# Four norms summed and rooted on four columns, tokens on partitions, in place of full 128x512 tiles

## The chip, the core and the metric

The kernel runs on one NeuronCore of one Trainium2 chip. The metric is the device time of one execution in microseconds (us). Before the change the median of three executions is 3365.46 us (3362.30 to 3369.93). The profiled execution itself took 3365.46 us, of which the profile's span covers 3363.7 us.

## What is computed

The reference is a stack of two equal layers and one further block over 512 tokens of width 1024, in float32. The change touches one place that each of the two layers passes once: the norms behind the attention heads.

```python
for i in range(DEPTH):                      # DEPTH = 2
    x = x + 0.5 * swiglu(rmsnorm(x, ffn1_norm[i]), ...)
    h = rmsnorm(x, mix_norm[i]) @ w_in[i]
    y_mla  = mla_mixer(...)                 # 8 heads, 512 channels out
    y_conv = silu(layernorm(depthwise_conv(u, 31 taps), ln_g, ln_b))   # 256 channels
    y_hy   = hyena_mixer(...)               # 256 channels
    y = concatenate([rmsnorm(y_mla, g[:512]), rmsnorm(y_conv, g[512:768]), rmsnorm(y_hy, g[768:])])
    x = x + y @ w_out[i]
    x = x + 0.5 * swiglu(rmsnorm(x, ffn2_norm[i]), ...)

def rmsnorm(x, g):
    return x * rsqrt(mean(x * x, axis=-1) + 1e-6) * g
```

So four norms stand here: the variance of the layer norm, and the mean squares of the hyena, the convolution and the attention outputs. In each, one number per token is needed, which is then applied to every channel of the token.

## The kernel before

Channels lie on the 128 partitions and the 512 tokens along the free axis: a tile is 128x512, and `y` has eight such tiles (0 and 1 convolution, 2 and 3 hyena, 4 to 7 attention). A sum over channels is thus a sum over partitions, which TensorE makes with a matrix of ones.

Each engine has its own program, written out by hand in its order; the only coupling is semaphores. `after(sem, k)` and `wait_ge` wait for a count. A wait holds everything that stands behind it on the same engine.

Weights come as 128x1024 blocks by DMA, GpSimd (POOL) splits each into a high and a low half (L452, L455), and TensorE multiplies in three passes (L506, L510, L511: `product`). `x_hi`/`x_lo` hold the two halves of the right-hand operand. `out_pair(half, pair)` is one such block of the output projection: 24 matmuls. Half 0 writes banks 4 to 7, half 1 banks 0 to 3. The pairs take, in turn, tiles 0 and 1 of the scaled hyena output (pair 0), the convolution (pair 1) and the attention (pairs 2 and 3) as `y_hi`, `y_lo`.

The order around the change, for one layer, on TensorE: the last part of head 6 with `conv_mean`; `hyena_sum` (two matmuls of the ones matrix with squared tiles, 128x512, into bank 0); `head(7, conv_variance, nothing)`, that is the two matmuls of the variance, then the transposes of the probabilities (`turn`, L800) and the products with the values (`mix`, L811); `run_idle(6)`, twelve matmuls whose result nobody reads (L859); `out_pair(0, 0)`; the sums of the convolution's and the attention's squares (`ones_sum`, L820, two and four matmuls); `out_pair(1, 0)`; and the six other pairs.

ScalarE squares the tiles, takes the square root of each 128x512 sum from its bank (`root`, L1428, and L1506) into `mix_rms` or `late_rms` (the memory of `key_rope`), copies the turned probabilities (`turned`, L1419), rounds scaled tiles to `y_hi` (`round_off`, L1434), and applies the SiLU of the convolution (L1513). Exponential, square root and SiLU need different function tables, and the table is loaded where the first user stands, behind that user's wait.

VectorE inverts the whole 128x512 root (`inverted`, L2116), scales (`scale_tiles`, L2105) and takes the remainders (`remainders`, L2111) that `out_pair` waits for by `norm_split`.

The same kernel already has, in its input projection, a narrow form of a norm: `latent_sums` (L891, data as the stationary operand against one column of ones, so that tokens come out on partitions, 128x4), a root and a reciprocal of 128x4, and `latent_spreads` (L899, an identity matmul of a broadcast column that spreads it back over a 128x128 square).

## Time and profile before

| | |
|---|---|
| median of 3 executions | 3365.46 us |
| profiled execution | 3365.46 us, span 3363.7 us |
| TensorE (PE) busy | 3224.4 us, 96% |
| VectorE (DVE) busy | 1827.7 us, 54% |
| ScalarE (ACT) busy | 739.2 us, 22% |
| GpSimd (POOL) busy | 1833.5 us, 55% |
| mean granted TensorE clock | 0.988 of full speed |

The busy share is an average over the whole span. The place that changes lies at 632 to 688 us for the first layer and at 1694 to 1750 us for the second. In the timeline a row is a run of like instructions: start, length, engine, line, operation, what it writes and reads, how many records, and in brackets how long the engine stood idle before it and for whom. A float32 matmul leaves two records. The granted clock is 1.00 for 2.4 GHz and 0.50 for 1.2 GHz.

### The profile page before, as it was taken

What the parts mean: (1) busy time and instruction counts of PE and PEld (TensorE: products, weight loads), DVE (VectorE), ACT (ScalarE), POOL (GpSimd) and SP (SyncE); (2) the same over time, 40 slices, a digit from 0 to 9 for tenths busy, and PEclk for the clock granted to TensorE, in tenths of its full rate; (3) what the DMA queues carried; (4) which work ended last, traced back from release to release, by engine and by line L of the source; (5) the groups of instructions that cost most, each with busy time, mean ns of one, the idle gap of its engine ahead of it and who ended that gap; (6) DMA issues with size and microseconds to landing.
All of it is one profiled execution on the core that took longest, in us unless ns stands there. A gap on an engine that the chain in (4) does not pass through costs nothing.

```text
span 3363.7 us, 44081 instructions
## 1 busy us (share of the span) xinstructions
PE 3224.4 (96%) x14534; PEld 2575.2 (77%) x14534; DVE 1827.7 (54%) x1997; ACT 739.2 (22%) x1248; POOL 1833.5 (55%) x1026
## 2 busy tenths in 40 slices
PE   8999998899999999998889999999999999999998
PEld 6788875578888778876557888788777877888886
DVE  7661378663313765138755331586768886753312
ACT  2110125422201111013532220112122322222200
POOL 5556651066666656653036666644455455666665
PEclk9999999999999999999999999999999999999999
DMA  4222320022333322231012232322222222223232
GB/s 159 76 88 94 113 82 20 12 83 96 97 96 103 111 76 92 96 112 51 13 38 94 94 100 94 122 76 68 64 85 69 76 69 70 94 92 96 97 97 81
DMA packets 77431, 281.26 MB, mean 84 GB/s; under 512 B 9383, under 2 KB 9767, under 8 KB 76777
## 3 DMA queue, kind: packets, MB, share of 16 engines
q1 hardware_dynamic: 74016, 268.58, 24.8%
q10 hardware_dynamic: 3272, 10.79, 0.9%
q8 instruction: 89, 1.46, 0.2%
q14 instruction: 54, 0.43, 0.0%
HBM read 277.24 MB, written 2.10 MB: 83 GB/s over the span
## 4 chain that ended last, share of the span: by engine, by line
PE 78%; DVE 15%; issue 4%; ACT 2%; DVEq 0%; DMA 0%; ACTq 0%; SPq 0%
PE bank L506 23%; PE bank L511 23%; PE bank L510 23%; DVE short L1926 1%; PE bank L641 1%; PE bank L726 1%; DVE x_lo L1706 1%; DVE y L1958 1%; DVE square_sum L1716 1%; DVE xbc L2267 1%; DVE scaled L2105 1%; PE bank L791 1%; PE bank L800 1%; DVE att_qk L2203 0%; DVE reach L2360 0%
## 5 line engine op out<-in xcount | busy, mean ns | idle before, releaser
L452 POOL TENSOR_SCALAR w_hi<-raw 128x1024 fp32r<-128x1024 f32 x504 | 555.6, 1102 | 1456.3 <-PE bank L506 1449.3
L455 POOL TENSOR_TENSOR w_lo<-raw,w_hi 128x1024 fp32r<-128x1024 f32 x504 | 1265.0, 2510 | 42.0
L506 PE MATMUL bank<-x_hi,w_hi 128*128 128x512 f32 x2896 | 1150.8, 397 | 48.7 <-DVE x_lo L1706 20.4
L511 PE MATMUL bank<-x_hi,w_lo 128*128 128x512 f32 x2896 | 1133.5, 391 | 0.0
L510 PE MATMUL bank<-x_lo,w_hi 128*128 128x512 f32 x2896 | 1132.9, 391 | 0.0
L506 PEld LDWEIGHTS bank<-x_hi,w_hi 128*128 128x128 f32 x2896 | 547.4, 189 | 184.2 <-issue 67.4
L510 PEld LDWEIGHTS bank<-x_lo,w_hi 128*128 128x128 f32 x2896 | 547.6, 189 | 114.7 <-issue 4.1
L511 PEld LDWEIGHTS bank<-x_hi,w_lo 128*128 128x128 f32 x2896 | 546.9, 189 | 115.6
L506 PE MATMUL bank<-hidden_hi,w_hi 128*128 (+1 forms) x880 | 342.3, 389 | 0.0
L511 PE MATMUL bank<-hidden_hi,w_lo 128*128 (+1 forms) x880 | 342.3, 389 | 0.0
L510 PE MATMUL bank<-hidden_lo,w_hi 128*128 (+1 forms) x880 | 342.3, 389 | 0.0
L1726 DVE SCALAR_TENSOR_TENSOR x<-bank,x 128x512 f32<-128x512 f32 x64 | 43.3, 687 | 547.6 <-PE bank L511 547.1
L1742 DVE TENSOR_TENSOR up<-bank,rstd 128x512 f32<-128x512 f32 x110 | 76.1, 692 | 338.7 <-PE bank L511 329.9
L1746 DVE TENSOR_TENSOR hidden_lo<-hidden,hidden_hi 128x512 f32 (+1 forms) x110 | 155.2, 1411 | 116.1 <-ACT hidden_hi L1275 116.1
L506 PEld LDWEIGHTS bank<-hidden_hi,w_hi 128*128 128x128 f32 x880 | 165.2, 188 | 34.6
L511 PEld LDWEIGHTS bank<-hidden_hi,w_lo 128*128 128x128 f32 x880 | 165.2, 188 | 34.3
L510 PEld LDWEIGHTS bank<-hidden_lo,w_hi 128*128 128x128 f32 x880 | 165.2, 188 | 34.0
L1275 ACT ACTIVATE hidden_hi<-hidden 128x512 f32 (+1 forms) x110 | 69.6, 633 | 432.5 <-DVE hidden L1744 432.5
L1259 ACT ACTIVATE x_hi<-x,gains 128x512 fp32r<-128x512 f32 x56 | 40.3, 720 | 516.5 <-DVE x L1726 516.2
L1744 DVE TENSOR_TENSOR hidden<-gate_silu,up 128x512 f32<-128x512 f32 x110 | 126.1, 1147 | 38.8 <-DVE up L1742 26.5
L1273 ACT ACT_TABLE_LOAD x68 | 87.2, 1283 | 239.5 <-DVE gate L1740 239.5
L1273 ACT ACTIVATE gate_silu<-gate 128x512 f32<-128x512 f32 x110 | 69.6, 633 | 218.2 <-DVE gate L1740 217.4
(383 smaller groups left out, 3228.4 us busy)
## 6 DMA issues: line engine op xcount, KB each, us to landing
raw<-in_w SPq DMA_DIRECT2D x504, 512.0 KB, 3.7
dft<-in_dft ACTq DMA_DIRECT2D x2, 1536.0 KB, 6.7
out<-x SPq DMA_DIRECT2D x4, 512.0 KB, 2.6
mask<-in_mask ACTq DMA_DIRECT2D x1, 1536.0 KB, 7.3
x<-in_x SPq DMA_DIRECT2D x2, 512.0 KB, 5.0
x<-in_x SPq DMA_DIRECT2D x1, 1024.0 KB, 7.4
filt_cos<-in_dft_filter ACTq DMA_DIRECT2D x2, 512.0 KB, 6.6
filt_sin<-in_dft_filter ACTq DMA_DIRECT2D x2, 512.0 KB, 7.8
```

The lines of the kernel that those rows point to most:

```text
L452: nc.gpsimd.tensor_scalar(w_hi[:, s % 2, :], raw[:, s, :], 1.0, 0.0, ALU.mult, ALU.add).then_inc(w_rounded, 1)
L455: nc.gpsimd.tensor_tensor(w_lo[:, s % 2, :], raw[:, s, :], w_hi[:, s % 2, :].bitcast(F32), ALU.subtract).then_inc(w_split, 1)
L506: first = nc.tensor.matmul(out, hi_w, hi, start=start, stop=False)
L510: nc.tensor.matmul(out, hi_w, lo, start=False, stop=False)
L511: return nc.tensor.matmul(out, lo_w, hi, start=False, stop=stop)
L1259: nc.scalar.activation(x_hi[:, m, :], x[:, m, :], ACT.Copy, scale=g).then_inc(x_rounded, 1)
L1273: nc.scalar.activation(gate_silu[:], gate[:], ACT.Silu).then_inc(gate_activated, 1)
L1275: nc.scalar.activation(to, hidden[:], ACT.Copy).then_inc(hidden_rounded, 1)
L1726: nc.vector.scalar_tensor_tensor(x[:, m, :], banks[b][:], coef, x[:, m, :], ALU.mult, ALU.add).then_inc(x_updated, c.add(x_updated))
L1742: link(nc.vector.tensor_tensor(up[:], bank[2 * b + 1][:], rstd[:], ALU.mult), pair_free)
L1744: link(nc.vector.tensor_tensor(hidden[:], gate_silu[:], up[:], ALU.mult), hidden_ready)
L1746: link(nc.vector.tensor_tensor(to_lo, hidden[:], to_hi.bitcast(F32), ALU.subtract), hidden_split)
```

## The change

The sums are made with the data as the stationary operand against one column of ones (`column_sums`), so that a sum is 128x4 and not 128x512. Root and reciprocal work on 128x4. Identity matmuls (`spread_root`) spread the reciprocal over a bank. For hyena and the layer norm VectorE reads that bank; for the two later norms ScalarE first copies the banks to `mix_rms` and `late_rms` (`root_taken`). The twelve idle matmuls go. Two one-element activations load the SiLU and the square root table at other places than before.

```diff
-        latent_root = sb("latent_root", [P, TT], F32, mix_mem)
+        latent_root = sb("latent_root", [P, 2 * TT], F32, mix_mem)
...
+            def column_sums(to, tiles):
+                for t in range(TT):
+                    for i, tile in enumerate(tiles):
+                        last = nc.tensor.matmul(bank[to][:, t:t + 1], tile[:, t * P:(t + 1) * P], ones[:, 0:1],
+                                                start=i == 0, stop=i == len(tiles) - 1)
+                return last
+
+            def spread_root(n, to, first=0):
+                after(latent_inverted, n)
+                for t in range(TT):
+                    last = nc.tensor.matmul(bank[to][:, t * P:(t + 1) * P],
+                                            latent_root[:, first + t:first + t + 1].broadcast_to([P, P]), ident[:],
+                                            start=True, stop=True)
+                last.then_inc(latent_spread, 1)
...
             def conv_variance():
                 after(ln_squared, 2)
-                ones_sum(HYENA_BANKS[0], conv_squares).then_inc(ln_sum, 1)
+                column_sums(HYENA_BANKS[0], conv_squares).then_inc(ln_sum, 1)
+                spread_root(3, HYENA_BANKS[1])
...
-                ones_sum(HYENA_BANKS[1], hyena_squares).then_inc(norm_sum, 1)
+                column_sums(HYENA_BANKS[1], hyena_squares).then_inc(norm_sum, 1)
...
-                head(7, conv_variance, nothing)
-
-                run_idle(6, SCORE_BANKS[0], probs_ready, 32)
+                head(7, conv_variance, lambda: spread_root(4, HYENA_BANKS[0]))
+
                 after(norm_split, 3 + 2)
-                after(norm_rms, 4)
+                after(probs_ready, 32)
                 out_pair(0, 0)
                 after(norm_squared, 3 + 7)
-                ones_sum(TURN_BANKS[0], conv_squares).then_inc(norm_sum, 1)
-                after(norm_squared, 3 + 5)
-                ones_sum(TURN_BANKS[1], mla_squares, 0, 3)
+                column_sums(TURN_BANKS[0], conv_squares).then_inc(norm_sum, 1)
                 after(norm_squared, 3 + 8)
-                ones_sum(TURN_BANKS[1], mla_squares, 3, 4).then_inc(norm_sum, 1)
+                column_sums(TURN_BANKS[1], mla_squares).then_inc(norm_sum, 1)
+                spread_root(5, TURN_BANKS[0])
+                spread_root(6, TURN_BANKS[1], TT)
                 after(mixed_copied, 8)
-                after(norm_rms, 6)
+                after(norm_rms, 8)
                 out_pair(1, 0)
...
-                def root(at, width, to):
-                    act.wait_ge(norm_sum, c.next(norm_sum))
-                    nc.scalar.activation(to[:], bank[at][:], ACT.Sqrt, bias=eps[:], scale=1.0 / width
-                                         ).then_inc(norm_rms, 1)
+                def root(at, width, done, first=0):
+                    act.wait_ge(done, c.next(done))
+                    nc.scalar.activation(latent_root[:, first:first + TT], bank[at][:, 0:TT], ACT.Sqrt, bias=eps[:],
+                                         scale=1.0 / width).then_inc(norm_rms, 1)
+
+                def root_taken(n, at, to):
+                    after(latent_spread, n)
+                    nc.scalar.activation(to[:], bank[at][:], ACT.Copy).then_inc(norm_rms, 1)
...
                 turned(7, 2)
                 turned(7, 3)
+                nc.scalar.activation(exp_warm[:], eps[:], ACT.Silu)
                 round_off([y_hi[k] for k in (0, 1)])
                 for i in range(CT):
                     act.wait_ge(norm_scaled, c.next(norm_scaled))
-                    nc.scalar.activation(y[:, i, :], scaled[:, i, :], ACT.Silu,
+                    nc.scalar.activation(y[:, i, :], y[:, i, :], ACT.Silu,
...
                 mla_square(3)
                 c.add(mixed_copied, 8)
-                root(TURN_BANKS[0], CW, mix_rms)
-                root(TURN_BANKS[1], T, late_rms)
+                nc.scalar.activation(exp_warm[:], eps[:], ACT.Sqrt)
+                root(TURN_BANKS[0], CW, norm_sum)
+                root(TURN_BANKS[1], T, norm_sum, TT)
+                root_taken(5, TURN_BANKS[0], mix_rms)
+                root_taken(6, TURN_BANKS[1], late_rms)
...
                 head(6, branches_done, hyena_done, centre)
-                inverted(mix_rms)
-                scale_tiles([y[:, 2 + i, :] for i in range(CT)], OUT_NORM + 2, mix_rms)
-                inverted(late_rms)
+                latent_inverse()
+                dve.wait_ge(latent_spread, c.next(latent_spread))
+                scale_tiles([y[:, 2 + i, :] for i in range(CT)], OUT_NORM + 2, bank[HYENA_BANKS[1]])
+                latent_inverse()
+                dve.wait_ge(latent_spread, c.next(latent_spread))
+                scale_centred()
                 remainders((0, 1))
-                scale_tiles([conv_acc[:, i, :] for i in range(CT)], LN_G, late_rms)
                 mixed(7)
+                latent_inverse()
+                latent_inverse(TT)
...
-                inverted(mix_rms)
+                dve.wait_ge(norm_rms, c.next(norm_rms))
                 scale_tiles([y[:, i, :] for i in range(CT)], OUT_NORM, mix_rms)
                 remainders((2, 3))
-                inverted(late_rms)
+                dve.wait_ge(norm_rms, c.next(norm_rms))
                 scale_tiles([y[:, 4 + i, :] for i in range(2)], OUT_NORM + 4, late_rms)
```

The first place is TensorE at the start of head 7. Before (L820 is `ones_sum`, L800 `turn`):

```order
L820 MATMUL bank<-square,ones 128x512 [waits norm_squared]
L820 MATMUL bank<-square,ones 128x512
L820 MATMUL bank<-short,ones 128x512 [waits ln_squared]
L820 MATMUL bank<-short,ones 128x512
L120 REGISTER_ALU
L800 MATMUL bank<-ident,probs 128x128 [waits probs_scaled]
```

And now (L854 is `column_sums`, L862 `spread_root`):

```order
L854 MATMUL bank<-ones,square 128x1 [waits norm_squared]
L854 MATMUL bank<-ones,square 128x1 x7
L854 MATMUL bank<-ones,short 128x1 [waits ln_squared]
L854 MATMUL bank<-ones,short 128x1 x7
L120 REGISTER_ALU
L862 MATMUL bank<-ident,latent_root 128x128 [waits latent_inverted]
L862 MATMUL bank<-ident,latent_root 128x128 x3
L120 REGISTER_ALU
L800 MATMUL bank<-ident,probs 128x128 [waits probs_scaled]
```

Two matmuls of 512 columns have become eight of one column, and a wait for VectorE with four identity matmuls now stands in front of the transposes.

The second place is TensorE ahead of the first pair of the output projection (L506). Before (L811 is `mix`, L859 `run_idle`):

```order
L811 MATMUL bank<-square,mla_v 64x256 [waits turned_copied]
L811 MATMUL bank<-square,mla_v 64x256
L859 MATMUL bank<-spectrum,ones 64x256 [waits probs_ready]
L859 MATMUL bank<-spectrum,ones 64x256 x11
L120 REGISTER_ALU
L120 ISA [waits norm_split]
L120 REGISTER_ALU [waits norm_rms]
L506 MATMUL bank<-x_hi,w_hi 128x512 [waits w_split]
```

And now:

```order
L862 MATMUL bank<-ident,latent_root 128x128 [waits latent_inverted]
L862 MATMUL bank<-ident,latent_root 128x128 x3
L120 REGISTER_ALU
L811 MATMUL bank<-square,mla_v 64x256 [waits turned_copied]
L811 MATMUL bank<-square,mla_v 64x256
L811 MATMUL bank<-square,mla_v 64x256 [waits turned_copied]
L811 MATMUL bank<-square,mla_v 64x256
L120 REGISTER_ALU
L120 REGISTER_ALU [waits norm_split,probs_ready]
L506 MATMUL bank<-x_hi,w_hi 128x512 [waits w_split]
```

The filler is gone, and the second spread stands between the last transposes and the last products.

The third place is TensorE between the first pair and the second. Before:

```order
L820 MATMUL bank<-short,ones 128x512 [waits norm_squared]
L820 MATMUL bank<-short,ones 128x512 x2
L120 REGISTER_ALU
L820 MATMUL bank<-short,ones 128x512 [waits norm_squared]
L120 REGISTER_ALU [waits mixed_copied]
L120 REGISTER_ALU [waits norm_rms]
L506 MATMUL bank<-x_hi,w_hi 128x512 [waits w_split]
```

And now:

```order
L854 MATMUL bank<-ones,short 128x1 [waits norm_squared]
L854 MATMUL bank<-ones,short 128x1 x15
L120 REGISTER_ALU
L862 MATMUL bank<-ident,latent_root 128x128 [waits latent_inverted]
L862 MATMUL bank<-ident,latent_root 128x128 x3
L120 REGISTER_ALU
L862 MATMUL bank<-ident,latent_root 128x128 [waits latent_inverted]
L862 MATMUL bank<-ident,latent_root 128x128 x3
L120 REGISTER_ALU [waits mixed_copied,norm_rms]
L506 MATMUL bank<-x_hi,w_hi 128x512 [waits w_split]
```

Ahead of both pieces stand the sums of the convolution, two matmuls before and eight now.

## Rows read from the trace of the kernel before

**Rows 1.** The page: busy times by engine, and the chain that ended last.

```profile
PE 3224.4 (96%) x14534; PEld 2575.2 (77%) x14534; DVE 1827.7 (54%) x1997; ACT 739.2 (22%) x1248; POOL 1833.5 (55%) x1026
...
PE 78%; DVE 15%; issue 4%; ACT 2%; DVEq 0%; DMA 0%; ACTq 0%; SPq 0%
```

**Rows 2.** Timeline of TensorE, layer one; the last row is layer two.

```profile
636.02 3.75 PE L820 MATMUL bank<-square,ones 128*128 128x512 f32 x4 [3.58 <-ACT square L1497]
639.56 2.86 PE L820 MATMUL bank<-short,ones 128*128 128x512 f32 x4
642.26 1.04 PE L800 MATMUL bank<-ident,probs 128*128 128x128 f32 x8
...
647.50 5.34 PE L859 MATMUL bank<-spectrum,ones 128*64 128x256 f32 x24
653.55 0.47 PE L506 MATMUL bank<-x_hi,w_hi 128*128 128x512 f32 x1 [0.71 <-DVE x_lo L2111]
...
659.08 5.31 PE L820 MATMUL bank<-short,ones 128*128 128x512 f32 x12
665.60 0.47 PE L506 MATMUL bank<-x_hi,w_hi 128*128 128x512 f32 x1 [1.21 <-ACT key_rope L1428]
...
673.11 0.47 PE L506 MATMUL bank<-x_hi,w_hi 128*128 128x512 f32 x1 [1.78 <-DVE x_lo L2111]
...
687.36 0.47 PE L506 MATMUL bank<-x_hi,w_hi 128*128 128x512 f32 x1 [3.11 <-DVE x_lo L2111]
...
1749.17 0.47 PE L506 MATMUL bank<-x_hi,w_hi 128*128 128x512 f32 x1 [3.09 <-DVE x_lo L2111]
```

**Rows 3.** Timeline of ScalarE, layer one.

```profile
639.89 1.28 ACT L1428 ACT_TABLE_LOAD   x1 [2.46 <-PE bank L820]
...
642.99 1.08 ACT L1419 ACTIVATE square<-bank 128x512 f32<-128x512 f32 x2 [1.12 <-PE bank L800]
...
646.75 1.20 ACT L1434 ACTIVATE x_hi<-scaled 128x512 fp32r<-128x512 f32 x2
653.93 1.28 ACT L1513 ACT_TABLE_LOAD   x1 [5.98 <-DVE scaled L2105]
```

**Rows 4.** Timeline of VectorE, layer one.

```profile
647.52 3.35 DVE L2116 RECIPROCAL key_rope<-key_rope 128x512 f32<-128x512 f32 x1 [0.33 <-DVE scaled L2105]
...
652.23 0.69 DVE L2111 TENSOR_TENSOR x_lo<-scaled,x_hi 128x512 fp32r<-128x512 f32 x1 [0.33 <-DVE x_lo L2111]
...
666.70 3.97 DVE L2105 SCALAR_TENSOR_TENSOR scaled<-y,layer_cols,mix_rms 128x512 f32<-128x512 f32 x2
```

**Rows 5.** Timeline, the narrow norm of the input projection, three engines.

```profile
432.76 0.26 ACT L1350 ACTIVATE latent_root<-bank,eps 128x4 f32<-128x4 f32 x1 [7.36 <-PE bank L891]
...
433.17 0.18 DVE L1931 RECIPROCAL latent_root<-latent_root 128x4 f32<-128x4 f32 x1 [1.12 <-ACT latent_root L1350]
...
447.43 1.02 PE L891 MATMUL bank<-ones,square_sum 128*128 128x1 f32 x8 [1.49 <-DVEq L1868]
453.89 1.05 PE L899 MATMUL bank<-ident,latent_root 128*128 128x128 f32 x8
```

**Rows 6.** Stretches: length, busy time by engine (count), granted clock, DMA share, GB/s.

```profile
636.00:642.30 6.30, 6.28 (x9) 2.68 (x10) 0.28 (x1) 3.40 (x5) 0.00 (x0) 0.56 0.01 3
647.70:653.50 5.80, 5.14 (x24) 3.01 (x22) 4.99 (x4) 0.25 (x1) 0.00 (x0) 1.00 0.00 0
2754.50:2755.00 0.50, 0.50 (x2) 0.33 (x1) 0.00 (x0) 0.00 (x0) 0.50 (x1) 0.50 0.00 0
```

**Rows 7.** Timeline of TensorE at other places where the clock is half.

```profile
560.25 0.76 PE L506 MATMUL bank<-x_hi,w_hi 128*128 128x512 f32 x1 [3.13 <-ACT probs L1407]
...
566.36 0.43 PE L511 MATMUL bank<-x_hi,w_lo 128*128 128x512 f32 x1
...
607.02 1.97 PE L800 MATMUL bank<-ident,probs 128*128 128x128 f32 x8
...
2752.83 1.02 PE L1184 MATMUL bank<-ones,square_sum 128*128 128x1 f32 x8 [1.29 <-DVEq L2397]
```

More of the change, by code:

```diff
@@ L105 @@
            "mixed_copied": 8, "spec_free": 4, "filt_loaded": 48, "odd_copied": 8, "spec_taken": 4,
-           "rope_ready": 4, "latent_inverted": 2, "latent_spread": 2, "latent_scaled": 2,
+           "rope_ready": 4, "latent_inverted": 6, "latent_spread": 6, "latent_scaled": 2,
            "positions_loaded": 16, "filt_sine": 4},
@@ L952, in mixer @@
                     out_pair(half, 3)
-                for sem_, k in ((norm_rms, 6), (norm_summed, 2), (norm_split, 11), (norm_squared, 11),
+                for sem_, k in ((norm_rms, 8), (norm_summed, 2), (norm_split, 11), (norm_squared, 11),
                                 (signal_ready, 2), (signal_timed, 4), (spec_free, 4), (out_spec_ready, 4),
@@ L956, in mixer @@
                                 (probs_ready, 32), (probs_scaled, 32), (turned_copied, 32), (mixed_copied, 8),
-                                (ln_in, 1), (ln_squared, 2), (latent_inverted, 2), (latent_scaled, 2)):
+                                (ln_in, 1), (ln_squared, 2), (latent_inverted, 6), (latent_scaled, 2)):
                     c.add(sem_, k)
@@ L1501, in mixer @@
                 mla_square(2)
-                root(HYENA_BANKS[1], CW, mix_rms)
+                root(HYENA_BANKS[1], CW, norm_sum)
                 turned(7, 0)
                 turned(7, 1)
-                act.wait_ge(ln_sum, c.next(ln_sum, 2))
-                nc.scalar.activation(late_rms[:], bank[HYENA_BANKS[0]][:], ACT.Sqrt, bias=eps[:], scale=1.0 / CW
-                                     ).then_inc(norm_rms, 1)
+                c.add(ln_sum)
+                root(HYENA_BANKS[0], CW, ln_sum)
                 turned(7, 2)
                 turned(7, 3)
+                nc.scalar.activation(exp_warm[:], eps[:], ACT.Silu)
                 round_off([y_hi[k] for k in (0, 1)])
@@ L1927, in short_tile, with latent_inverse @@
                                                             short[:, i, :], ALU.mult, ALU.add))
-                def latent_inverse():
+                def latent_inverse(first=0):
                     dve.wait_ge(norm_rms, c.next(norm_rms))
-                    nc.vector.reciprocal(latent_root[:], latent_root[:]).then_inc(latent_inverted, c.add(latent_inverted))
+                    own = latent_root[:, first:first + TT]
+                    nc.vector.reciprocal(own, own).then_inc(latent_inverted, c.add(latent_inverted))
                 def latent_scale(tiles, at):
@@ L2106, in scale_tiles, with scale_centred @@
                                                             ALU.mult, ALU.mult), norm_scaled)
+                def scale_centred():
+                    for i in range(CT):
+                        link(nc.vector.scalar_tensor_tensor(y[:, i, :], y[:, i, :], col(LN_G + i),
+                                                            bank[HYENA_BANKS[0]][:], ALU.mult, ALU.mult), norm_scaled)
                 def remainders(tiles):
@@ L2112, in remainders @@
                                                      ALU.subtract), norm_split)
-                def inverted(rms):
-                    dve.wait_ge(norm_rms, c.next(norm_rms))
-                    link(nc.vector.reciprocal(rms[:], rms[:]))
                 for i in (2, 0, 1):
```

14 lines of the change are left out of this document (8 added, 6 removed).

## The prediction

> **What bounds the kernel now.** I read the page first: TensorE is busy 96% of the span, and 78% of the last chain is its own work [rows 1]. So only time in which TensorE stands still, works at half clock, or does work that can go is worth anything. Next I read TensorE's timeline around the change, and took from each row the bracket that says for whom it waited. From the hyena sums at 636.02 to the seventh block of the output projection at 687.36 it loses time in five places [rows 2]: at half clock in the first sums, ahead of the first pair (653.55), ahead of the second (665.60), and ahead of two later pairs (1.78 and 3.11 us for a remainder of VectorE). Then I asked ScalarE and VectorE what they did meanwhile: a table load of 1.28 us [rows 3] and reciprocals of 3.35 us [rows 4], one behind the other. Last the granted clock, in stretches [rows 6]. Layer two shows the same waits (3.09 us where layer one has 3.11 [rows 2]), so I reckon one layer and double it.
>
> **The change part by part, for one layer.**
>
> *a. Up to the first pair.* The chain was: sums, table load, root, reciprocal 3.35, scaling, second reciprocal 3.35, remainders, pair at 653.55 [rows 2 to 4]. Root and reciprocal shrink to 0.26 and 0.18 us [rows 5], some 7 us less on VectorE. But TensorE gets more to do. A short sum: eight records take 1.02 us [rows 5]; take the last one's 0.25 off, and it is 0.11 us a record. The hyena sum has 16 records, that is 1.8 us at full clock. The trace does not show such records at half clock: from below they cost the same 0.11, from above twice that, 0.22 (wide transposes do double: 1.97 against 1.04 us for eight [rows 7, 2]). The clock is at half from before 636 until about 641.5 (0.56 over 6.3 us [rows 6]), and I take the upper end: 16 x 0.22 = 3.5 us, as long as the two wide matmuls (636.02 to 639.56 [rows 2]). The variance sums then end at 643.1 instead of 642.3, if the clock is still half; the spread stands behind them (1.05 us for eight records at full clock [rows 5], 1.8 at half) and in front of the transposes, which therefore start at 644.8, not 642.26. The wait of this spread costs little: load 1.28, root 0.26 and reciprocal 0.18 fit beside the variance sums. What is queued behind it is all of head 7.
>
> Now the other side. The last transposes end near 649.5; ScalarE copies (1.08 for two), loads the SiLU table (1.28, formerly hidden in a wait of 5.98), rounds two tiles (1.20) [rows 3]; VectorE subtracts (0.69 each, 0.33 between [rows 4]); 0.6 us later the pair starts, as before. That gives 654.8. With the cheap records and full clock from the transposes on, the same sum gives 652.5. The old start lies between. I take 653.6: **0 us, ends -1.0 and +1.2**. The two reciprocals are thus gone, and what is late instead is the head's own transposes, a table load, and the copies.
>
> The Trainium skill ("ScalarE: Activation LUTs", What ACT_TABLE_LOAD costs) adds about 1.38 us of draining to each 1.28 us load. Rows 3 show the load alone at 1.28 and the root right behind it; by the skill the pair would start 1.4 us later.
>
> *b. The filler is gone.* The twelve idle matmuls ran 5.34 us, and the clock stayed 1.00 over them [rows 2, 6]. Now TensorE is idle from the last product, about 2.6 to 3.2 us, until the pair. Rows 7 show what such a gap can do: after 3.13 us idle the block at 560.25 ran at half clock until 566.36, 14 matmuls with 0.20 us more each, 2.8 us. Yet after 3.11 us at 687.36 the next matmul takes the full-clock 0.47 [rows 2]. So 0 to 2.8; the gap here follows light work, as at 560, so I take **+2.2 us**.
>
> *c. Between first and second pair.* Before: 12 wide records and the root, 659.08 to 665.60, 6.52 us [rows 2]. Now 16 + 32 short records (48 x 0.11 = 5.3), then root 0.26, reciprocal 0.18 and four hops of about 0.15 beside the first spread, the second spread (1.0 after it), the second copy of ScalarE (0.6) and a hop: 8.0 us. That is +1.5 at full clock. The loads are hidden here (SQRT is loaded under the first pair). At half clock from somewhere in the sums on: two spreads cost 1.7 more and the remaining sums up to 0.9; from below nothing. In the later block the clock falls to 0.50 right behind eight such records after a gap of 1.29 [rows 6, 7]. Nothing in the trace shows forty-eight of them in a row. I take half clock in their last part: +1.5 + 2.1 = **+3.6 us, ends +1.5 and +6.5** (all at half clock).
>
> *d. The second pair* then starts at half clock: 0 to 2.8 as in b; **+1.6 us**.
>
> *e. The later waits.* From 665.60 to 687.36 are 21.76 us for three pairs of 24 matmuls at 0.227 us (5.45): 16.35. So 5.4 us are lost there. VectorE's chain begins at the first copy of ScalarE, no later in relation to the pair than before, and has no 3.35 in front; its first scalings, 3.97 us for two [rows 4], should be shorter, since they now fall ahead of GpSimd's next split; the second 3.35 goes too. The remainders of tiles 4 to 7 come about 15.5 us after its start, one pair ahead of need. **-5.4 us**; what is late next is nothing: POOL's 3.7 us per block stay below a pair.
>
> Sum: 0 + 2.2 + 3.6 + 1.6 - 5.4 = +2.0 us a layer, +4.0 for two. On the profiled execution's 3365.5 us (span 3363.7 and 1.8 around it; it is also the median) that is **3369.5 us**, 0.12% more: within what a measurement of this kernel can tell from no change, which I set at 0.2%, 6.7 us.
>
> **Rivals.**
>
> *Full clock throughout.* a -1.0, b 0, c +1.5, d 0, e -5.4: -4.9 a layer, 3355.7 us. For it: 3.11 us idle left the clock up at 687. Against: the clock fell behind short sums in the later block [rows 6, 7], and the filler that stood in the way is removed. 14%.
>
> *Only the first gap costs clock.* 0 + 2.2 + 1.5 + 0 - 5.4 = -1.7, 3362.1 us. It needs the short sums to keep the clock up. 20%.
>
> *The head too runs at half clock.* Slower than before: the place is head 7, behind 32 short records. There the old wide matmuls brought the clock back at about 641.5; if the new ones don't, transposes and products run at the rate of 607.02, 8 records in 1.97 instead of 1.04 [rows 7, 2]: two groups of transposes and two of products, 1 us each, less what was slow already, +3 in a; b +2.8, c +5, d +2.8, e -5.4: +8.2 a layer, 3381.9 us. It decides from the point where the clock does not return before the last transposes. Against: at 607 the clock came back behind transposes and scores. 22%. The skill's "TensorE: Matmul & The Clock Gate" (Part 4: PE-mode transpose) says that full clock doesn't engage for transposes; by it this case would be the likely one. Rows 7 show eight transposes at half clock and do not settle it.
>
> *The waits of e stay*, because ScalarE's second copy stands ahead of the round-offs: only 3 of the 5.4 us go, +4.4 a layer, 3374.3 us. For it: ScalarE is strictly in order. Against: the copy is 0.6 us, and there is a pair of slack. 4%.
>
> **How the numbers follow.** My forecast has 40%: it needs half clock in the sums between the pairs, and its own range is 3363 to 3376. Slower by more than 0.2% (over 3372.2): all of the half-clock head, most of the staying waits, and a quarter of the forecast's own case: 0.36. Faster by more than 0.2% (under 3358.7): the full-clock case and some of the third: 0.17. The rest 0.47. The range 3358 to 3381 leaves out most of the first rival and the upper part of the third.
>
> **What would show it.** In the changed profile: the start of the first pair against 653.55; the granted clock in the stretch of the sums, in head 7 and in the first two pairs; the distance from first to second pair against 12.05; and no wait ahead of the third and the seventh pair. If the clock is 1.00 from 642 to 670, the forecast is too high by b, d and half of c. If the short records cost 0.22 at full clock as well, it is too low.

## The result and the profile after

| | before | after |
|---|---|---|
| median | 3366.69 us (20 runs, 3362.3 to 3374.69) | 3372.67 us (20 runs, 3367.85 to 3377.98) |
| ratio | | 1.0015, 95% interval 1.0009 to 1.0021 |
| profiled execution | 3365.5 us, span 3363.7 | 3367.85 us, span 3366.1 |
| mean granted clock | 0.988 | 0.984 |

The change makes the kernel slower by some 5 us (0.15%, interval 3 to 7). That is clear of zero, but under the 0.2% that I had set as what can be told from no change; the forecast was +4.0 us. The page of the kernel after answers to [rows 1]:

```profile
PE 3236.1 (96%) x14670; PEld 2601.0 (77%) x14670; DVE 1801.4 (54%) x1997; ACT 738.7 (22%) x1256; POOL 1833.4 (54%) x1026
```

VectorE has 26 us less to do and the span is none the shorter: TensorE is busy 12 us more. The rest is in the details. Here is the timeline of TensorE after, layer one (start, duration, engine, line, operation, count, idle time before it and what ended it); it answers to [rows 2]:

```profile
635.70 2.31 PE L854 MATMUL bank<-ones,square 128*128 128x1 f32 x16 [3.58 <-ACT square L1517]
637.87 3.55 PE L854 MATMUL bank<-ones,short 128*128 128x1 f32 x16
641.28 2.05 PE L862 MATMUL bank<-ident,latent_root 128*128 128x128 f32 x8
643.13 1.91 PE L800 MATMUL bank<-ident,probs 128*128 128x128 f32 x8
...
647.21 1.12 PE L800 MATMUL bank<-ident,probs 128*128 128x128 f32 x8
...
653.60 0.47 PE L506 MATMUL bank<-x_hi,w_hi 128*128 128x512 f32 x1 [3.36 <-DVE x_lo L2141]
...
660.75 6.94 PE L854 MATMUL bank<-ones,short 128*128 128x1 f32 x48
667.55 3.76 PE L862 MATMUL bank<-ident,latent_root 128*128 128x128 f32 x16
...
672.43 0.47 PE L506 MATMUL bank<-x_hi,w_hi 128*128 128x512 f32 x1 [1.12 <-ACT key_rope L1449]
...
689.84 0.47 PE L506 MATMUL bank<-x_hi,w_hi 128*128 128x512 f32 x1 [0.81 <-DVE x_lo L2141]
```

The reader sees one short record cost 0.22 us where it follows others at half clock (16 in 3.55), and 48 of them take 6.94 us, a mean of 0.145: they begin at full clock and lose it on the way. The spread behind them, 16 records, takes 3.76 us, 0.235 each; at full clock 8 took 1.05 [rows 5]. Idle time shows at three places now: 3.36 us ahead of the first pair (there is no filler any more), 1.12 ahead of the second, 0.81 ahead of the fifth, at 689.84. (From 672.43 to here run the second, the third and the fourth pair. The block at 687.36 that the prediction calls the seventh [rows 2] is the fifth as well.) The wait ahead of the third pair is gone.

The same stretch by windows (length, busy time of TensorE, its weight loads, VectorE, ScalarE and GpSimd with counts, granted clock, DMA share, GB/s):

```profile
635.70:641.28 5.58, 5.58 (x32) 5.58 (x33) 0.18 (x1) 2.96 (x5) 0.00 (x0) 0.62 0.01 3
641.28:649.15 7.87, 7.61 (x41) 5.98 (x41) 1.67 (x3) 2.46 (x6) 0.00 (x0) 0.62 0.00 0
650.10:653.60 3.50, 0.14 (x3) 0.03 (x1) 2.44 (x5) 3.49 (x8) 0.00 (x0) 1.00 0.00 0
653.60:660.75 7.15, 7.15 (x24) 5.71 (x25) 0.56 (x2) 2.45 (x4) 3.41 (x2) 0.76 0.24 74
660.75:672.43 11.68, 10.56 (x65) 10.29 (x64) 1.86 (x4) 2.11 (x5) 0.00 (x0) 0.71 0.00 1
672.43:689.84 17.41, 16.60 (x72) 13.44 (x73) 14.04 (x10) 3.20 (x6) 11.46 (x6) 1.00 0.23 71
```

Read the clock column: half (1.2 GHz) for most of the sums and well into head 7, back to full (2.4 GHz), half again within the first pair, full by its end, half again from somewhere within the sums between the pairs, and full through the next 17.41 us. The three falls don't stand behind the same thing. The first comes about 1.3 us into the first sums, behind 3.58 us of idle time (granted clock 1.00 over the first microsecond, 0.68 over the next); the kernel before has half clock there too, with its wide sums [rows 6], so the single column did not make this one. The second has a gap ahead of it, 3.36 us. The third has none: TensorE was busy without a break at full clock, and it falls in the middle of the one-column sums.

Four distances carry the comparison from here on. H runs from the start of the hyena sums to the first pair, P1 from there to the next sums, C from the sums to the second pair, W from the second to the fifth pair. In us, layer one and layer two of the one profiled execution of each kernel:

| kernel | H | P1 | C | W | total |
|---|---|---|---|---|---|
| before | 17.53, 17.62 | 5.53, 5.52 | 6.52, 6.67 | 21.76, 21.74 | 51.34, 51.55 |
| after | 17.90, 17.94 | 7.15, 7.17 | 11.68, 11.67 | 17.41, 17.39 | 54.14, 54.17 |
| difference | +0.37, +0.32 | +1.62, +1.65 | +5.16, +5.00 | -4.35, -4.35 | +2.80, +2.62 |

Both layers together: +5.42 us, as much as the ratio says (0.0015 of 3367 us is 5.1; the medians differ by 6.0). (The two spans differ by 2.4 only, for elsewhere the profiled execution after happened to be 3 us shorter: from the fifth pair of layer one to the hyena sums of layer two 1007.64 us against 1010.26. The code there is the same. This execution is the fastest of the twenty.)

### The profile page after: what moved, and what is told of

Read it like the earlier page. It is cut to its first block, busy times and chain, and to the rows that moved or that the text cites. A ratio compares the mean times of both kernels' runs of the same rounds, so it can differ in the third digit from the quotient of the medians.

```text
span 3366.1 us, 44367 instructions
## 1 busy us (share of the span) xinstructions
PE 3236.1 (96%) x14670; PEld 2601.0 (77%) x14670; DVE 1801.4 (54%) x1997; ACT 738.7 (22%) x1256; POOL 1833.4 (54%) x1026
## 3 DMA queue, kind: packets, MB, share of 16 engines
q10 hardware_dynamic: 3272, 10.79, 1.0%
## 4 chain that ended last, share of the span: by engine, by line
PE 79%; DVE 15%; issue 4%; ACT 2%; DVEq 0%; DMA 0%; ACTq 0%; SPq 0%
PE bank L506 23%; PE bank L511 23%; PE bank L510 23%; DVE short L1950 1%; PE bank L641 1%; PE bank L726 1%; DVE x_lo L1730 1%; DVE y L1983 1%; PE bank L854 1%; DVE square_sum L1740 1%; DVE xbc L2298 1%; PE bank L800 1%; DVE x_lo L2141 1%; PE bank L791 1%; DVE att_qk L2234 0%
## 5 line engine op out<-in xcount | busy, mean ns | idle before, releaser
L455 POOL TENSOR_TENSOR w_lo<-raw,w_hi 128x1024 fp32r<-128x1024 f32 x504 | 1266.2, 2512 | 42.0
L506 PE MATMUL bank<-x_hi,w_hi 128*128 128x512 f32 x2896 | 1151.2, 397 | 45.7 <-DVE x_lo L1730 20.9
L506 PEld LDWEIGHTS bank<-x_hi,w_hi 128*128 128x128 f32 x2896 | 547.8, 189 | 179.4 <-issue 62.5
L506 PE MATMUL bank<-hidden_hi,w_hi 128*128 (+1 forms) x880 | 342.3, 389 | 0.0
L506 PEld LDWEIGHTS bank<-hidden_hi,w_hi 128*128 128x128 f32 x880 | 165.2, 188 | 34.6
```

Source lines behind the costliest of these rows:

```text
L455: nc.gpsimd.tensor_tensor(w_lo[:, s % 2, :], raw[:, s, :], w_hi[:, s % 2, :].bitcast(F32), ALU.subtract).then_inc(w_split, 1)
L506: first = nc.tensor.matmul(out, hi_w, hi, start=start, stop=False)
```

## The experiments

Each was timed beside the kernel before, on the same chip. Of the expectations only the numbers per layer can be compared closely; a ratio's interval is about 0.001 to each side, 3 us.

**The filler back, between head 7 and the first pair.** This asks whether the gap is what costs the 1.6 us in P1.

```diff
                 head(7, conv_variance, lambda: spread_root(4, HYENA_BANKS[0]))
 
+                run_idle(3, SCORE_BANKS[0], probs_ready, 32)
                 after(norm_split, 3 + 2)
-                after(probs_ready, 32)
                 out_pair(0, 0)
```

> The changed kernel with six idle matmuls back between the last products of head 7 and the first pair (twelve records, about 2.7 us in a gap of 3.36). If the gap makes the clock fall (our theory of term b), the first pair runs at granted clock 1.00 and takes 5.53 us again instead of 7.15, its start stays within 0.2 us of 17.9 us behind the hyena sums: -1.6 us a layer, -3.2 us on the whole, ratio to the kernel before about 1.0006. If the clock falls whatever fills the gap (rival), the time stays at 1.0015.

Measured: 3366.57 us, ratio to before 0.9994 (0.9985 to 1.0003). TensorE, layer one, then the two stretches behind:

```profile
653.02 2.75 PE L875 MATMUL bank<-spectrum,ones 128*64 128x256 f32 x12
...
656.40 0.47 PE L506 MATMUL bank<-x_hi,w_hi 128*128 128x512 f32 x1 [0.62 <-DVE x_lo L2141]
661.97 7.38 PE L854 MATMUL bank<-ones,short 128*128 128x1 f32 x48
```

```profile
656.40:661.97 5.57, 5.57 (x25) 4.58 (x26) 0.71 (x2) 2.60 (x4) 3.45 (x2) 1.00 0.09 13
661.97:674.09 12.12, 11.00 (x66) 10.74 (x64) 1.86 (x4) 2.11 (x5) 0.00 (x0) 0.63 0.10 39
```

The pair takes 5.57 us at clock 1.00 in both layers. So P1 is the gap's price, 1.6 us a layer, and the filler pays. It does nothing for C, which is 12.12 and 10.05 here: the loss between the pairs is another one. In layer one the second pair even began at half clock (W 18.65), which is what my term d had feared. The ratio is better than the 1.0006 that I had expected, and the distances give less of it (+0.9 us against before, where the ratio gives -2.0): the profiled execution, 3372.02 us, is the slowest of the eleven.

**The sums with 128 columns instead of one.** The same 80 records a layer, the same weight loads, the same order; only the moving operand is as wide as a spread's. The root reads every 128th column.

```diff
-                        last = nc.tensor.matmul(bank[to][:, t:t + 1], tile[:, t * P:(t + 1) * P], ones[:, 0:1],
+                        last = nc.tensor.matmul(bank[to][:, t * P:(t + 1) * P], tile[:, t * P:(t + 1) * P], ones[:],
...
-                    nc.scalar.activation(latent_root[:, first:first + TT], bank[at][:, 0:TT], ACT.Sqrt, bias=eps[:],
+                    nc.scalar.activation(latent_root[:, first:first + TT], bank[at][:, 0:T:P], ACT.Sqrt, bias=eps[:],
```

> The changed kernel with the sums made against all 128 columns of ones instead of one column: the same count of instructions and weight loads, the same inputs, 128 columns instead of one through the array, and ScalarE reads every 128th column. Theory A (the one-column matmuls are what lets the clock fall): granted clock 1.00 in the 48-record stretch, from its start to the second pair 8 to 8.5 us instead of 11.68; in head 7 the clock comes back before the transposes, so that these and the products take about 1.0 us a group instead of 1.9 and the first pair starts up to 2 us earlier: -4 to -5 us a layer, -8 to -10 us on the whole, ratio to before about 0.999. Rival B (the gaps and hops around the sums do it, or the extra columns cost as much as they save): no change against the changed kernel beyond 0.5 us a layer, ratio 1.0015.

Measured: 3361.33 us, ratio 0.9978 (0.9969 to 0.9987). TensorE, layer one, and the stretches:

```profile
640.37 3.15 PE L854 MATMUL bank<-ones,short 128*128 128x128 f32 x16
643.35 1.06 PE L862 MATMUL bank<-ident,latent_root 128*128 128x128 f32 x8
...
660.39 5.52 PE L854 MATMUL bank<-ones,short 128*128 128x128 f32 x48
665.75 2.16 PE L862 MATMUL bank<-ident,latent_root 128*128 128x128 f32 x16
```

```profile
643.35:648.89 5.54, 4.86 (x42) 4.06 (x40) 1.67 (x3) 2.35 (x6) 0.00 (x0) 1.00 0.00 0
660.39:669.02 8.63, 7.51 (x65) 7.21 (x64) 1.55 (x4) 2.11 (x5) 0.00 (x0) 1.00 0.03 14
```

This settles the largest term. With 128 columns the clock stays at 1.00 over all 48 records and the spreads, and C falls from 11.68 to 8.63 in both layers; H falls from 17.90 to 15.26. The clock fell there with 128 columns too, about 1.4 us into the first sums (sixteen records in 2.50 us), but it was back at about 642.9, before the spread; in the kernel after it came back only at 647.3, in the second transposes. So in H the single column delays the return and does not make the fall. A record takes 0.115 us (5.52 / 48), about the 0.11 that I had read for one column at full clock [rows 5]: 127 more columns are free. With only the columns different, the sums of one column cost 5.7 us a layer more (2.64 in H, 3.05 in C). P1 stays 7.05, for the gap is still there.

**The SiLU table loaded late again.** The prediction had put this load on the path to the first pair. Here the activation that called for it early is taken out, so that the load falls behind the first two round-offs.

```diff
                 turned(7, 3)
-                nc.scalar.activation(exp_warm[:], eps[:], ACT.Silu)
                 round_off([y_hi[k] for k in (0, 1)])
```

> The changed kernel without the one-element SiLU ahead of the round-offs, so that the table is loaded at the first real SiLU again. If the load lies on the path to the first pair (term a as predicted), the round-offs move 1.4 us earlier and the pair starts up to 1.3 us earlier, -2.6 us on the whole. Rival, which the trace of the changed kernel speaks for (the first remainder starts 0.33 us behind the scaling of the centred tiles, which ends at 651.01): VectorE is as late as ScalarE there, and the pair starts 0 to 0.3 us earlier; the whole within 0.6 us of the changed kernel, ratio 1.0013 to 1.0015.

Measured: 3374.1 us, ratio 1.0017 (1.0008 to 1.0026), the same as the change; H is 17.90 and 17.94, to a hundredth what it was. ScalarE, and then VectorE, of this kernel:

```profile
649.43 1.15 ACT L1454 ACTIVATE x_hi<-scaled 128x512 fp32r<-128x512 f32 x2
650.67 1.28 ACT L1532 ACT_TABLE_LOAD   x1
```

```profile
649.81 1.64 DVE L2134 SCALAR_TENSOR_TENSOR y<-y,layer_cols,bank 128x512 f32<-128x512 f32 x2 [3.10 <-PE bank L862]
651.78 0.69 DVE L2140 TENSOR_TENSOR x_lo<-scaled,x_hi 128x512 fp32r<-128x512 f32 x1 [0.33 <-DVE y L2134]
```

ScalarE has both roundings done by 650.6, and still the first remainder starts at 651.78, because two scalings stand ahead of it on VectorE (1.64 us) and wait for the second spread of TensorE. My theory of the load on the path falls: it has a rival of equal length beside it, and taking one of the two away gives nothing.

**The new norms in the first part only.** The hyena norm and the layer norm narrow, the two behind the first pair wide as before, with their two wide reciprocals.

```diff
-                column_sums(TURN_BANKS[0], conv_squares).then_inc(norm_sum, 1)
+                ones_sum(TURN_BANKS[0], conv_squares).then_inc(norm_sum, 1)
...
-                spread_root(5, TURN_BANKS[0])
-                spread_root(6, TURN_BANKS[1], TT)
```

> Only the first half of the change: hyena norm and layer norm on four columns, filler gone, SiLU table early, while the two later norms keep their wide sums, roots and reciprocals. By our terms it keeps a (+0.4) and b (+1.6) and drops c (+5.2) with d and e (-4.4): +2.0 us a layer, +4.0 on the whole, ratio to before 1.0012. Rival (the first half is neutral and the second carries the loss): ratio 1.0000 to 1.0003.

Measured: 3371.71 us, ratio 1.0006 (0.9997 to 1.0015), which holds both expectations. The distances say more: C is back at 6.67 (wide sums hold the clock), W is 20.22 in both layers, between 21.76 before and 17.41 after, and layer one and layer two differ in a way worth a look. TensorE, layer one, then the first pair of layer two:

```profile
654.96 0.47 PE L506 MATMUL bank<-x_hi,w_hi 128*128 128x512 f32 x1 [3.36 <-DVE x_lo L2148]
...
660.52 5.31 PE L820 MATMUL bank<-short,ones 128*128 128x512 f32 x12
...
687.41 0.63 PE L506 MATMUL bank<-x_hi,w_hi 128*128 128x512 f32 x1 [3.10 <-DVE x_lo L2148]
...
1717.86 0.47 PE L506 MATMUL bank<-x_hi,w_hi 128*128 128x512 f32 x1 [3.36 <-DVE x_lo L2148]
...
1718.82 0.63 PE L506 MATMUL bank<-x_hi,w_hi 128*128 128x512 f32 x1
```

The gap is 3.36 us in either layer. In layer one the pair then took 5.56 us (654.96 to 660.52), at full clock throughout; in layer two it fell to 0.63 us a matmul and took 7.16. And behind the 3.10 us ahead of the fifth pair the clock was at half here (0.63), while behind 3.11 us at the same place it was not in the kernel before [rows 2]; this cost nine matmuls and 1.6 us that lie behind W and so in none of the four distances. So a gap of this length goes either way, and one profile of it is one draw. In the five kernels with the 3.36 us ahead of the first pair, ten passes in all, eight paid for it (P1 7.05 to 7.17) and two did not (5.56, 5.83).

W has something more to say. The later norms are wide here as before, with their reciprocals of 3.35 us, and still the wait ahead of the third pair is 0.25 us, not 1.78. VectorE of this kernel, then GpSimd of the kernel before:

```profile
666.86 1.65 DVE L2133 SCALAR_TENSOR_TENSOR scaled<-y,layer_cols,mix_rms 128x512 f32<-128x512 f32 x2
```

```profile
667.40 2.71 POOL L455 TENSOR_TENSOR w_lo<-raw,w_hi 128x1024 fp32r<-128x1024 f32 x1
```

The same two scalings took 3.97 us before [rows 4], from 666.70 to 670.67, and GpSimd's split from 667.40 to 670.11 lies within them. Here they are over by 668.51, and the same step of GpSimd (L455) begins at 669.51. They start 0.33 us ahead of the second pair instead of 1.10 behind it, as the table of the square root is loaded under the first pair (at 656.32) and no longer behind the sums. So 1.5 us of what the change gains in W stand here without the narrow later norms. That the earlier load is the reason is read from these rows; no run has it alone.

**The first tiles rounded and subtracted early.** Since H has two limits of equal length, this takes both away: ScalarE's first two round-offs move ahead of the copy of the last turned head, and VectorE's two remainders ahead of its scaling of the centred tiles. The fourth spread goes to the bank that the third used.

```diff
-                head(7, conv_variance, lambda: spread_root(4, HYENA_BANKS[0]))
+                head(7, conv_variance, lambda: spread_root(4, HYENA_BANKS[1]))
...
+                round_off([y_hi[k] for k in (0, 1)])
                 turned(7, 2)
                 turned(7, 3)
                 nc.scalar.activation(exp_warm[:], eps[:], ACT.Silu)
-                round_off([y_hi[k] for k in (0, 1)])
...
-                                                            bank[HYENA_BANKS[0]][:], ALU.mult, ALU.mult), norm_scaled)
+                                                            bank[HYENA_BANKS[1]][:], ALU.mult, ALU.mult), norm_scaled)
...
+                remainders((0, 1))
                 dve.wait_ge(latent_spread, c.next(latent_spread))
                 scale_centred()
-                remainders((0, 1))
```

> The changed kernel with the round-offs of tiles 0 and 1 on ScalarE moved ahead of the last two copies of head 7 (it is idle there for 2.1 us), the remainders on VectorE ahead of the scaling of the centred tiles, and the second spread into the bank that the first used. Then the remainders are ready at about 648.7 and the first pair follows the last products at once, near 650.4 instead of 653.6: -3.2 us a layer, and with no gap ahead of it the pair runs at full clock, -1.6 more; what lies behind it moves along. -4.8 us a layer, -9 to -10 on the whole, ratio to before 0.9986 to 0.9990. Rival: the squares and the table load for the later sums are now late, so that half of this comes back between the pairs: ratio 0.9998 to 1.0005.

Measured: 3362.52 us, ratio 0.9983 (0.9974 to 0.9992). TensorE of this kernel, layer one:

```profile
650.56 1.08 PE L811 MATMUL bank<-square,mla_v 128*64 128x256 f32 x8
651.58 0.50 PE L506 MATMUL bank<-x_hi,w_hi 128*128 128x512 f32 x1
```

No wait and no gap: the pair follows the last products, P1 is 5.57 and 5.59 with the clock at full, without a filler. H is 13.30 and 15.43 against 17.90 (in layer two the clock was at half from the first sum on, sixteen records in 3.55 us). C stays 11.68 in layer one and 10.58 in layer two, for the one-column sums are unchanged.

**The squares added on VectorE first.** The other way to hold the clock up between the pairs is to have fewer sums: VectorE, idle there, adds the two convolution squares and the four of the attention, and TensorE has 16 records instead of 48. (`add_mla_squares(n, tiles)` adds each of the tiles to the first one, once n squares are there.)

```diff
+                add_mla_squares(5, (1, 2))
+                after(norm_squared, 7)
+                link(nc.vector.tensor_tensor(conv_squares[0], conv_squares[0], conv_squares[1], ALU.add))
+                dve.sem_inc(norm_summed, 1)
+                add_mla_squares(8, (3,))
+                dve.sem_inc(norm_summed, 1)
...
-                column_sums(TURN_BANKS[0], conv_squares).then_inc(norm_sum, 1)
+                column_sums(TURN_BANKS[0], conv_squares[:1]).then_inc(norm_sum, 1)
...
-                column_sums(TURN_BANKS[1], mla_squares).then_inc(norm_sum, 1)
+                column_sums(TURN_BANKS[1], mla_squares[:1]).then_inc(norm_sum, 1)
```

> The changed kernel with the squares of the convolution and of the attention added up on VectorE first (it is idle there), so that the sums between the first pairs take 16 records instead of 48. Theory A: 16 x 0.11 = 1.8 us, the clock stays at 1.00, and root, reciprocal and spreads make it 4.5 to 5 us from the first sum to the second pair instead of 11.68: -6.8 us a layer, of which up to 2 come back as a wait ahead of the later pairs, since VectorE then has less time for tiles 4 to 7. -10 to -13 us on the whole, ratio to before 0.998. Rival: the additions are not done by the end of the first pair and the wait for them takes the gain: ratio 1.0005 or more.

Measured: 3362.57 us, ratio 0.9987 (0.9978 to 0.9996). TensorE, layer one:

```profile
659.32 1.84 PE L854 MATMUL bank<-ones,short 128*128 128x1 f32 x16
661.13 2.02 PE L862 MATMUL bank<-ident,latent_root 128*128 128x128 f32 x16
...
682.55 0.47 PE L506 MATMUL bank<-x_hi,w_hi 128*128 128x512 f32 x1 [1.67 <-DVE x_lo L2146]
```

C is 4.95 in layer one, as expected, at clock 1.00. In layer two it is 6.22, for there the clock fell after all (0.72 over the stretch, and the second pair began at half clock, its first matmul 0.76 us). So sixteen one-column records may cost the clock too. Part of the gain comes back as a wait: W rises from 17.41 to 18.28 in layer one, since the pairs come sooner and the remainders of VectorE don't; 1.67 us ahead of the fifth pair instead of 0.81.

**Both of these, and both with 128 columns.** The last two kernels put the edits together, the second also with the wide operand.

> Both of the former together. If the gains add: -4.8 and -6.8 with 2 to 4 us of new waits ahead of the later pairs, about -8 us a layer, -16 on the whole, ratio to before 0.9965 to 0.9975. Rival: with the first pair 3 us earlier the additions on VectorE end behind it, and no more than 3 us a layer come on top of the better one: ratio about 0.998.

> The same as the last with the sums against 128 columns of ones. If one-column matmuls let the clock fall (theory A), head 7 gets its clock back earlier and its transposes and products take about 1.0 us a group instead of 1.9: 1 to 3 us a layer less than the last, ratio about 0.9955 to 0.997. If the number of columns does not matter: equal to the last within 0.5 us a layer.

Measured: 3354.45 us, ratio 0.9966 (0.9954 to 0.9979), and 3347.29 us, ratio 0.9941 (0.9927 to 0.9954). Both are faster than the kernel before. The first is where it was expected. The second is 21 us under the 3368.33 of the kernel before in its comparison, and faster than I had expected (0.9955 to 0.997). TensorE of it, layer one, and two stretches:

```profile
639.54 2.02 PE L854 MATMUL bank<-ones,square 128*128 128x128 f32 x16 [3.59 <-ACT square L1517]
641.40 1.95 PE L854 MATMUL bank<-ones,short 128*128 128x128 f32 x16
...
662.64 0.47 PE L506 MATMUL bank<-x_hi,w_hi 128*128 128x512 f32 x1 [1.12 <-ACT key_rope L1449]
```

```profile
639.54:644.67 5.13, 4.77 (x41) 4.61 (x42) 0.18 (x1) 2.96 (x5) 0.00 (x0) 1.00 0.01 3
657.28:662.64 5.36, 4.24 (x32) 3.79 (x33) 2.25 (x5) 2.11 (x5) 0.00 (x0) 1.00 0.02 7
```

The clock is 1.00 in both. In layer one it did not fall after the 3.59 us ahead of the first sums either; in layer two it did (2.71 and 2.94 us for the two sixteens). That is 1.04 us of H, luck of the draw as far as one profile tells. The other part of the surplus is in W, 17.3 in both layers against 18.6 and 18.4 in the kernel without the wide operand. With one column the clock fell in C of layer one (5.70), and the second pair began at half clock there. In layer two it did not fall (5.26), but the first two remainders of VectorE behind the start of the second pair took 1.51 and 2.48 us there, and here 0.69 and 1.12.

The distances of all kernels, beside what the comparison of times gave (before is 0; both layers together):

| kernel | H | P1 | C | W | by distances | by ratio |
|---|---|---|---|---|---|---|
| after | 17.90, 17.94 | 7.15, 7.17 | 11.68, 11.67 | 17.41, 17.39 | +5.4 | +5.1 |
| filler back | 16.71, 17.75 | 5.57, 5.56 | 12.12, 10.05 | 18.65, 17.40 | +0.9 | -2.0 |
| 128 columns | 15.26, 15.26 | 7.05, 7.05 | 8.63, 8.63 | 17.40, 17.39 | -6.2 | -7.4 |
| SiLU table late | 17.90, 17.94 | 7.13, 7.17 | 11.68, 11.67 | 17.37, 17.39 | +5.4 | +5.7 |
| first part only | 16.78, 17.90 | 5.56, 7.16 | 6.67, 6.67 | 20.22, 20.22 | -1.7 | +2.0 |
| early round-off | 13.30, 15.43 | 5.57, 5.59 | 11.68, 10.58 | 17.38, 18.52 | -4.8 | -5.7 |
| squares added | 17.90, 16.84 | 7.13, 5.83 | 4.95, 6.22 | 18.28, 18.00 | -7.7 | -4.4 |
| both | 15.50, 14.46 | 6.94, 6.95 | 5.70, 5.26 | 18.61, 18.44 | -11.0 | -11.5 |
| both, 128 columns | 10.79, 11.83 | 6.95, 6.95 | 5.36, 5.35 | 17.29, 17.32 | -21.1 | -19.9 |

The last column is the ratio less one, times 3367 us, and uncertain by about 3 us (4 in the last two rows). The two columns agree within 4 us everywhere, so the stretch holds the effect as far as these uncertainties can tell; the largest difference, 3.7 us, is that of the first part only, where 1.6 us lie just behind W. In the last two kernels P1 contains 1.2 us of waiting for VectorE's additions ahead of the sums; the pair itself ran at full clock.

## Why the prediction was right

The forecast was 3369.5 us, +4.0, and the kernel is some 5 us slower. The mechanism is the one that was forecast: VectorE's time goes, later waits go, and the longer stretch between the pairs and the clock of TensorE take it all back. Term by term, for layer one:

| step | predicted | measured |
|---|---|---|
| a, up to the first pair | 0 | +0.37 |
| b, filler gone | +2.2 | +1.62 |
| c, between the pairs | +3.6 | +5.16 |
| d, second pair at half clock | +1.6 | 0 |
| e, later waits | -5.4 | -4.35 |
| sum | +2.0 | +2.80 |

That the sum lies within 0.8 us is in part luck. The terms are off by +0.37, -0.58, +1.56, -1.6 and +1.05, and c and d cancel: together they were forecast at 5.2 and measured at 5.16. The slow time behind the sums is there as foreseen, but all of it lies before the second pair.

*a held, but for one wrong reason.* The variance sums ended at 641.3, not 643.1, as the clock was still at full in the first records (sixteen in 2.31 us) and the sums began 0.3 earlier; the transposes began at 643.1, not 644.8. Then transposes and products ran at half clock for longer than forecast (1.91 us for eight transposes, 1.12 for the next eight). The table load, which the prediction put on the path, isn't on it (the run with the late table). What it had overlooked is that VectorE must scale the two centred tiles first:

```profile
649.37 1.64 DVE L2135 SCALAR_TENSOR_TENSOR y<-y,layer_cols,bank 128x512 f32<-128x512 f32 x2 [3.12 <-PE bank L862]
651.34 0.69 DVE L2141 TENSOR_TENSOR x_lo<-scaled,x_hi 128x512 fp32r<-128x512 f32 x1 [0.33 <-ACT x_hi L1454]
...
680.51 2.47 DVE L2141 TENSOR_TENSOR x_lo<-scaled,x_hi 128x512 fp32r<-128x512 f32 x1 [0.33 <-DVE x_lo L2141]
...
686.29 2.13 DVE L2141 TENSOR_TENSOR x_lo<-scaled,x_hi 128x512 fp32r<-128x512 f32 x1 [0.68 <-DVE scaled L2130]
```

ScalarE of the kernel after shows the load in what is in effect spare time; it answers to [rows 3]:

```profile
648.02 1.08 ACT L1435 ACTIVATE square<-bank 128x512 f32<-128x512 f32 x2 [2.10 <-PE bank L800]
649.13 1.28 ACT L1529 ACT_TABLE_LOAD   x1
650.42 0.20 ACT L1529 ACTIVATE exp_warm<-eps 128x1 f32<-128x1 f32 x1
```

The copies end at 649.10, the load starts at 649.13, takes 1.28 us, and the next activation starts 0.01 us behind it. The draining of about 1.38 us that the Trainium skill ("ScalarE: Activation LUTs", What ACT_TABLE_LOAD costs) adds to a load is not to be seen on either side of this one, and the pair was not 1.4 us late.

*b held* (inside 0 to 2.8). The filler run shows the gap as its cause, and the run with the first part only shows that it need not be paid each time.

*c is the term that was mis-sized.* The step that was off is "I take half clock in their last part: +1.5 + 2.1". Here are its stretches in the kernel after:

```profile
660.75:664.40 3.65, 3.65 (x35) 3.64 (x33) 0.18 (x1) 0.26 (x1) 0.00 (x0) 1.00 0.01 3
664.40:667.55 3.15, 3.15 (x16) 3.15 (x17) 0.00 (x0) 0.00 (x0) 0.00 (x0) 0.50 0.00 0
```

The clock was half behind about 33 of the 48 records, and stayed so to the end of the spreads. Against the 128-column run (C 8.63), that cost 3.05 us in layer one (1.4 in the sums, 6.94 against 5.52, and 1.6 in the spreads, 3.76 against 2.16), where I had put 2.1. And at full clock the stretch is 8.63 long, not 8.0, so the +1.5 is +2.1. Both parts were too small: +5.16, between my +3.6 and the upper end of +6.5. What I had right is where the loss comes from, and the 128-column run shows its cause to be the single column. The other runs agree: with 48 one-column records the clock fell before the second pair in all eight passes (C 10.05 to 12.12, four kernels), with 128 columns in none of four (two of these with 16 records).

*d was 0*, and for a reason that the prediction didn't see: the clock came back at about 671.1, as the spreads ended, and the second pair started at full clock, with 0.47 us. It is a matter of where the return falls. In layer one of the filler run it fell late, and d was there (W 18.65 against 17.40 in its layer two, 1.25). The early round-off in layer two, the added squares in layer two and both together in layer one began the second pair at half clock as well (0.76 or 0.77 us for its first matmul).

*e was -4.35 instead of -5.4.* The wait ahead of the third pair went entirely, of the one ahead of the fifth 0.81 us stayed. The prediction gave two reasons, the missing reciprocals and first scalings ahead of GpSimd's split; for the third pair the second is enough, as the run with the first part only shows, which has the wide reciprocals. The remainders of the last tiles were ready 19.0 us after the start of VectorE's scalings (670.48 to 689.45), not 15.5. The rows of VectorE above show why: a remainder is 0.69 us where GpSimd stands still, and 2.47 and 2.13 where it splits weights. The scalings for tiles 4 to 7 are longer too: 3.44 and 2.48 us for two, where two took 1.65 behind the sums. GpSimd of the same kernel at that time:

```profile
679.73 2.70 POOL L455 TENSOR_TENSOR w_lo<-raw,w_hi 128x1024 fp32r<-128x1024 f32 x1
...
685.16 2.72 POOL L455 TENSOR_TENSOR w_lo<-raw,w_hi 128x1024 fp32r<-128x1024 f32 x1
```

The remainder of 680.51 ends at 682.98, 0.55 us behind the split that began at 679.73; the one of 686.29 ends at 688.42, 0.54 behind the other. Each looks as if it had waited for the split and then run. The Trainium skill ("SBUF — State Buffer", SBUF: two separate sides) describes just that: a VectorE operation with two inputs in SBUF and one of GpSimd exclude each other for a whole instruction. The trace agrees, with these ends, and so does the pair of rows from the run with the first part only; no run here took the splits away.

Of the rivals, full clock throughout and only the first gap are out: the one-column sums cost the clock in both layers of after. The head at half clock, the slow one, came half true. The clock did stay half through one group of transposes (1.91 us) and one of products, and then came back, so that the second transposes took 1.12 us. So the rule of the Trainium skill named in the prediction ("TensorE: Matmul & The Clock Gate", Part 4: PE-mode transpose), by which this would have been the likely case, isn't borne out by head 7: with 128 columns the clock was 1.00 over all its transposes and products (643.35 to 648.89). The page says it of the transpose mode, and the records, plain MATMUL rows, don't show whether that mode was on. That the waits of e stay is out as well.

What stays open: whether a gap of 3.1 to 3.6 us costs the clock differs from execution to execution and from layer to layer, and so it does for sixteen one-column records (two of four passes); nothing here says what decides it. Open too is why the single column costs the clock, and how much of the last kernel's surplus is a lucky draw.

## What to carry to other kernels

When a reduction over partitions is turned round so that its result is narrow, keep the moving operand wide: a record of 128 columns took the same 0.11 us as one of a single column, and left TensorE at full clock for what came behind it. Time saved on an engine that isn't the bound is worth only the waits of the bounding engine that go with it, and what the change adds on the bounding engine comes off that: here 4.35 us of waits went in a layer, and 7.15 came. Three edits each turned the loss into a gain by themselves (128 columns 0.9978, early round-off 0.9983, added squares 0.9987), and together they gave 0.9941. And a thing "on the path" may have a neighbour of equal length: look at what the waiting instruction has ahead of it on each engine, not at the longest item alone.

## What was unexpected of the hardware

- One column cost the clock, 128 columns kept it, with the same number of records and weight loads: 6.94 against 5.52 us for 48, 3.76 against 2.16 us for the 16 spreads behind. The cause of it is not shown.
- The same idle time gave either clock: 3.36 us ahead of the first pair of the run with the first part only, full in layer one (5.56 us for the pair) and half in layer two (7.16).
- A subtraction of 128x512 on VectorE took 0.69 us alone and up to 2.47 beside a weight split of GpSimd.
